# Attention of a hybrid decoder trunk: 20 slots of one head pair become 13 slots of one or two pairs, with the mask buffers at another address

## The chip, the cores and the metric

One core of one Trainium2 chip runs the whole program. The metric is the device time of one execution in microseconds (us).

## What is computed

The reference is a decoder trunk of two layers on 512 tokens of width 1024, in float32. A layer is a SwiGLU feed-forward half step, a mixer of three parallel groups of heads, and a second SwiGLU half step:

```python
x = x + 0.5 * swiglu(rms_norm(x, ffn1_norm[l]), ...)
h = rms_norm(x, mix_norm[l])
(dq, dk, dv, iq, ik, iw, gq, gk, gv, gz, ga, gb, mq) = split_columns(h @ w_in[l])
out_a = dsa_attention(qa, ka, va, q_idx, ik, w_idx, rel_bias)   # 6 heads x 64, top 128 keys, causal, relative bias
out_b = gdn_mixer(gq, gk, gv, gz, ga, gb, ...)                  # 6 heads x 64, gated delta rule
out_c = memory_attention(mq, mem_kv, ...)                       # 4 heads x 64, 256 memory tokens
x = x + concat(out_a, out_b, out_c) @ w_out[l]
x = x + 0.5 * swiglu(rms_norm(x, ffn2_norm[l]), ...)
```

This case is about the stage in which out_a and out_c are computed (logits, softmax, product with the values), and the product with w_out that runs beside it.

## The kernel before

**Float32 products.** Large products are made of three matmuls of rounded operands: weights and activations are split in a high part (wh, XH) and a low part (wl, XL), and the helper `three` issues high*high, high*low and low*high (lines 932 to 934). A unit of weights (1 MB) is loaded into raw[0] or raw[1] by SyncE, rounded into wh (by ScalarE, line 1463, and for two units of this stage by GpSimd, line 899, in halves of 128x1024), and VectorE makes wl from raw and wh (line 1838 for halves).

**The order.** Each engine walks the same list, MIX_ORDER, and issues its own part of each step in that order; semaphores tie the engines together. `_order` writes the list. The attention stage is its last part: steps ("att", slot), between them steps of the output product ("rd", r, c, i: one `three` of 128x512 for output block c), additions of a finished output block to the residual ("ex", line 2152 on VectorE), rounds of the top-k selection of the last token block ("sel", lines 1934 to 1939 on VectorE), and halves of weight splits ("hi" and "lo"). `_early` spreads the first two groups of rounds over the slots, and after the last slot TAIL has the remaining 24 rounds. FIRST_ROUNDS use the results of the delta rule (gzT, split by the "gsplit" steps: XH on ScalarE, line 1696, XL on VectorE, line 2085), SECOND_ROUNDS need those of the memory heads, LAST_ROUNDS those of the masked heads.

**The slots.** A job is one head of one block of 128 queries; a pair is two jobs. There are 8 pairs of memory heads (256 keys each), then 12 pairs of masked heads: three each for blocks 0 to 3, with 128, 256, 384 and 512 keys. Pair p passes through the slots as a pipeline:

- slot p: TensorE makes the logits (line 1384) of both heads in two PSUM banks (0 and 1; 6 and 7 for p = 1); VectorE takes the row maxima (line 2111 for memory heads; line 2107, a fused add of the mask and minimum, for the others).
- slot p+1: ScalarE takes the exponential (line 1712) with the row sum; VectorE inverts the sum (line 2124).
- slot p+2: TensorE transposes the probabilities (line 1359) into banks 2 and 5, ScalarE copies them to pT (line 1729); GpSimd spreads the inverse sums (`spread`, rwide, line 873).
- slot p+3: TensorE transposes rwide (line 1369) and multiplies the values with pT (line 1395), both into bank 3; ScalarE copies both to oA (line 1738).
- slot p+4: GpSimd multiplies them (`normalise`, oN, line 865); where a block is complete, ScalarE (line 1719) and VectorE (line 2118) split it into XH and XL.

The masks of masked heads (`combine`, line 892, comb) are made by GpSimd two slots ahead, in four buffers that share their place with the values and keys of the memory heads, so that the first of them waits for the last memory product (`pool.wait_ge(S["jv_done"], M_JOBS)`).

On TensorE the parts of one slot follow each other as: transposes of pair slot-2, transpose of rwide of pair slot-3, logits of pair slot (these wait until the exponentials or maxima of the pair before are done), values of pair slot-3, then the rounds.

Of the kernel before, what the change touches and what calls it, by code (L numbers as in the profile page):

```python
# [8 lines left out]
F32 = mybir.dt.float32  # L9
# [140 lines left out]
N_SLOTS = N_PAIRS + 4  # L150
IDX_BATCHES = 6

# [8 lines left out]
def _early():  # L161
# [24 lines left out]
def logits_bank(p):  # L186

    return 6 if p == 1 else 0
# [10 lines left out]
def _order():  # L199
# [143 lines left out]
    for p in range(N_SLOTS):  # L343
        order.append(("att", p))
# [5 lines left out]
        if p == 1:  # L350
            pull(9.0)
            put(("hi", 16, 0, KD // 2))
# [8 lines left out]
        if 5 <= p <= 12:  # L361
            sel(1)
        put(*EARLY.get(p, ()))
# [12 lines left out]
                  os_ps=4, os_read=4, or_done=4, op_done=4, jr_done=N_PAIRS, jo_done=N_PAIRS, jx_done=N_PAIRS, jb_done=N_PAIRS, og_done=4, gh_done=3, gl_done=3, cb_done=18, tap_done=9, pr_done=24, ex_done=16, hf_hi=3, hf_lo=3,  # L376
# [28 lines left out]
def job(n):  # L405

    return (n // H_M, H_A + n % H_M) if n < M_JOBS else ((n - M_JOBS) // H_A, (n - M_JOBS) % H_A)


# [9 lines left out]


def masked_count(b, j):

    return H_A * (b - 1) + j + 1
# [113 lines left out]
def hybrid_trunk(nc, xt, memt, cols, strip_table, weights, consts, out):  # L537
    depth = cols.shape[1]

    with ExitStack() as ctx:  # L540
# [37 lines left out]
        with ExitStack() as third:  # L578
            comb = [sb(f"comb{i}", [P, T], F32, third) for i in range(4)]
# [20 lines left out]
        sb("behind_gcol", [P, NB, H_B])  # L600
        beta, gdec, bg, kdec, tmpa, tmpb, tmpc = (gcol[:, i] for i in range(7))
        m8 = sb("m8", [P, 8])
        mxs = sb("mxs", [P, 4])
# [9 lines left out]
        with ExitStack() as third:  # L613
            pT = [sb(f"pT{i}", [P, T], F32, third) for i in range(2)]
# [6 lines left out]
        with ExitStack() as third:  # L621
            at = [sb(f"at{i}", [P, T], F32, third) for i in range(4)]
            pT += [sb(f"pT{i}", [P, T], F32, third) for i in range(2, 4)]
# [16 lines left out]
        with ExitStack() as third:  # L640
            oA = sb("oA", [P, 2, 2, P], F32, third)
            rwide = sb("rwide", [P, 2, 2, DH], F32, third)
            oN = sb("oN", [P, 2, 3, P], F32, third)
# [63 lines left out]
        with nc.Block() as block:  # L707
# [56 lines left out]
            def _(pool):  # L764
                def layer(L):
# [90 lines left out]
                    def normalise(p):  # L856

                        if 0 <= p < N_PAIRS:
                            b, j = job(2 * p)
                            done = phase(2 * p)[2]  # L860
                            c = (j if j < H_A else j - H_A) // 2
                            if c == 0 and done > 1:
                                pool.wait_ge(S["o_lo"], done - 1)
                            pool.wait_ge(S["jo_done"], of("jo_done", p + 1))
                            pool.tensor_tensor(oN[:, done % 2, c, :], oA[:, p % 2, 0, :], oA[:, p % 2, 1, :], ALU.mult
                                               ).then_inc(S["jx_done"], 1)

                    def spread(p):

                        if 0 <= p < N_PAIRS:  # L870
                            b, j = job(2 * p)
                            pool.wait_ge(S["jr_done"], of("jr_done", p + 1))
                            pool.tensor_copy(rwide[:, p % 2], rrec[:, b % 2, j:j + 2].unsqueeze(2).to_broadcast([P, 2, DH])
                                             ).then_inc(S["jb_done"], 1)

                    def combine(p):

                        for n in (2 * p, 2 * p + 1):
                            if n >= N_JOBS:
                                return  # L880
                            b, j = job(n)
                            if b and j < H_A:
                                m = masked_count(b, j)
                                w = P * (b + 1)
                                if m == 1:
# [6 lines left out]
                                pool.tensor_tensor(comb[(m - 1) % 4][:, 0:w], strips[j][:, T - w:], unsel[b][:, :],  # L892
# [27 lines left out]
            def _(pe):  # L920
                def layer(L):
# [170 lines left out]
                    def out_round(r, c, i):  # L1092
# [13 lines left out]
                        if early:  # L1106
                            nth_bank = KD * (rounds is SECOND_ROUNDS) + n
                            dst = bank[early_bank(c, rounds is SECOND_ROUNDS)]
                            if (r, i) in STARTS and nth_bank in (1, 2):
                                pe.wait_ge(S["je_done"], 4)  # L1110
                            if (r, i) in STARTS and nth_bank >= 3:
                                pe.wait_ge(S["ex_done"], of("ex_done", nth_bank - 2))
                        else:
                            dst = bank[n]
                            if (r, i) in STARTS:
                                if n in (0, 1):
                                    pe.wait_ge(S["o_lo"], 2 * NB)
                                    pe.wait_ge(S["je_done" if n == 0 else "jm_done"], N_JOBS)
                                elif n in (2, 5):
                                    pe.wait_ge(S["jp_even" if n == 2 else "jp_odd"], N_PAIRS)  # L1120
# [226 lines left out]
                    def attention(slot):  # L1347
                        p = slot - 2
                        if 0 <= p < N_PAIRS:
                            for e in range(2):  # L1350
                                n = 2 * p + e
                                b, j = job(n)
                                if n == 0:
                                    wait_copied(N_GROUPS - 1)
# [909 lines left out]
```

## Time and profile before

| | |
|---|---|
| median of 3 runs | 2112.43 us (2112.2 to 2112.84) |
| the profiled execution: time | 2112.39 us |
| its span, first to last instruction | 2110.6 us |
| granted TensorE clock over the span | 1.000 |
| attention stage, first logits to the last two rounds before TAIL, layer 1 | 601.76 to 681.11 us |
| the same, layer 2 | 1649.52 to 1728.86 us |

The profile page gives busy times of each engine and the costliest groups; the timeline lists instructions in order, `x4` being four of a kind merged in one row, with the idle time of the engine in front of it and what ended that in brackets. PE is TensorE's matmuls, PEld its weight loads, DVE VectorE, ACT ScalarE, POOL GpSimd. Ends of matmuls are modelled, so distances between starts are what is read for them. A float32 logits, value or transpose product is issued as passes: two rows for one logits or value matmul, one for one transpose.

### The profile page before, as it was taken

The numbers are of one execution on the slowest core, as the hardware profiler recorded it, in microseconds if no ns is written. First come the engines' busy times: TensorE is split into PE (matmuls) and PEld (weight loads), VectorE is DVE, ScalarE is ACT, GpSimd is POOL, SyncE is SP. The second block draws the span as 40 slices with busy tenths as digits, with TensorE's granted clock in tenths as the row PEclk, the third lists the DMA queues.
The fourth block names the chain that finished last, engine by engine and source line by source line (L and its number), as shares of the span: only waits on it lengthen the run. The fifth ranks groups of instructions, "written<-read, shape, count | busy, mean of one in ns | idle before, by whom it ended". The sixth has DMA issues, their size and how long they took to land.

```text
span 2110.6 us, 31901 instructions
## 1 busy us (share of the span) xinstructions
PE 2084.5 (99%) x13097; PEld 1676.8 (79%) x13097; DVE 1034.0 (49%) x1421; ACT 775.9 (37%) x1096; POOL 393.9 (19%) x373
## 2 busy tenths in 40 slices
PE   9999999999999999999999999999999999999999
PEld 7888888877766888888888888887777668888887
DVE  5433333688766533433333433336887665334322
ACT  5222222475546422222232222224755554222211
POOL 1110011105035501101111110121051355111000
PEclk9999999999999999999999999999999999999999
DMA  5222222322111222222222222223212112222222
GB/s 194 87 96 99 95 90 95 127 84 72 47 69 38 100 99 99 99 95 90 95 100 99 99 99 93 93 103 113 80 62 92 41 41 100 99 99 86 94 105 75
DMA packets 30646, 192.41 MB, mean 91 GB/s; under 512 B 3216, under 2 KB 5392, under 8 KB 11984
## 3 DMA queue, kind: packets, MB, share of 16 engines
q1 hardware_dynamic: 30160, 189.80, 25.8%
q8 instruction: 77, 1.26, 0.2%
q10 hardware_dynamic: 384, 1.14, 0.1%
q14 instruction: 25, 0.20, 0.0%
HBM read 188.70 MB, written 2.10 MB: 90 GB/s over the span
## 4 chain that ended last, share of the span: by engine, by line
PE 85%; DVE 8%; ACT 4%; issue 2%; POOL 1%; DMA 0%; SPq 0%; DVEq 0%; ACTq 0%; POOLq 0%
PE psum L932 27%; PE psum L934 26%; PE psum L933 26%; DVE wl L1838 1%; PE psum L1384 1%; PE psum L1395 1%; ACT wh L1463 1%; PE psum L1248 1%; PE psum L1245 1%; PE psum L1359 1%; DVE acc L1921 1%; POOL comb L892 1%; DVE wrk L1936 1%; DVE XL L1853 1%; DVE m L1934 1%
## 5 line engine op out<-in xcount | busy, mean ns | idle before, releaser
L932 PE MATMUL psum<-XH,wh 128*128 128x512 f32 x1904 | 756.3, 397 | 4.9 <-DVE XL L1798 2.2
L933 PE MATMUL psum<-XL,wh 128*128 128x512 f32 x1904 | 741.9, 390 | 0.0
L934 PE MATMUL psum<-XH,wl 128*128 128x512 f32 x1904 | 741.8, 390 | 0.0
L932 PEld LDWEIGHTS psum<-XH,wh 128*128 128x128 f32 x1904 | 357.2, 188 | 103.2 <-issue 24.7
L934 PEld LDWEIGHTS psum<-XH,wl 128*128 128x128 f32 x1904 | 357.4, 188 | 75.6
L933 PEld LDWEIGHTS psum<-XL,wh 128*128 128x128 f32 x1904 | 357.6, 188 | 70.5 <-issue 1.0
L1846 DVE TENSOR_TENSOR wl<-raw,wh 128x2048 fp32r<-128x2048 f32 x88 | 201.7, 2292 | 159.4 <-ACT wh L1468 159.4
L932 PE MATMUL psum<-HH,wh 128*128 128x512 f32 x704 | 273.9, 389 | 0.0
L933 PE MATMUL psum<-HL,wh 128*128 128x512 f32 x704 | 273.9, 389 | 0.0
L934 PE MATMUL psum<-HH,wl 128*128 128x512 f32 x704 | 273.9, 389 | 0.0
L1463 ACT ACTIVATE wh<-raw 128x2048 fp32r<-128x2048 f32 (+1 forms) x84 | 157.3, 1872 | 305.5 <-PE psum L934 305.5
L779 POOL TENSOR_TENSOR sg<-sg,rF 128x512 f32<-128x512 f32 x88 | 113.6, 1293 | 783.5 <-ACT sg L1493 783.5
L1824 DVE TENSOR_TENSOR wl<-raw,wh 128x2048 fp32r<-128x2048 f32 x52 | 122.1, 2347 | 251.3 <-ACT wh L1463 251.2
L1499 ACT ACTIVATE HH<-hf 128x512 f32 (+1 forms) x88 | 55.6, 632 | 328.3 <-DVE hf L1875 328.3
L1468 ACT ACTIVATE wh<-raw 128x2048 fp32r<-128x2048 f32 x88 | 167.4, 1902 | 13.1 <-PE psum L934 13.1
L1493 ACT ACTIVATE sg<-sg 128x512 f32<-128x512 f32 x88 | 55.2, 631 | 292.9 <-DVE sg L1867 292.9
L1867 DVE TENSOR_TENSOR sg<-psum,rF 128x512 f32<-128x512 f32 x88 | 60.1, 687 | 193.5 <-PE psum L934 172.1
L933 PEld LDWEIGHTS psum<-HL,wh 128*128 128x128 f32 x704 | 132.1, 188 | 27.5
L934 PEld LDWEIGHTS psum<-HH,wl 128*128 128x128 f32 x704 | 132.1, 188 | 27.5
L932 PEld LDWEIGHTS psum<-HH,wh 128*128 128x128 f32 x704 | 132.1, 188 | 27.3
L1875 DVE TENSOR_TENSOR hf<-sg,psum 128x512 f32<-128x512 f32 x88 | 60.5, 687 | 134.2 <-PE psum L934 125.8
L701 POOL TENSOR_TENSOR sg<-xT 128x512 f32<-128x512 f32 x40 | 47.8, 1197 | 358.9 <-DVE xT L1890 333.4
(255 smaller groups left out, 1980.1 us busy)
## 6 DMA issues: line engine op xcount, KB each, us to landing
raw<-weights SPq DMA_DIRECT2D x143, 1024.0 KB, 4.8
raw<-weights SPq DMA_DIRECT2D x32, 896.0 KB, 4.4
xT<-xt SPq DMA_DIRECT2D x4, 512.0 KB, 6.3
memT<-memt SPq DMA_DIRECT2D x2, 1024.0 KB, 4.9
out<-xT SPq DMA_DIRECT2D x8, 256.0 KB, 6.0
stripsA<-strip_table SPq DMA_DIRECT2D x2, 768.0 KB, 6.6
raw<-weights SPq DMA_DIRECT2D x2, 512.0 KB, 6.6
stripsB<-strip_table SPq DMA_DIRECT2D x2, 512.0 KB, 7.0
```

The costliest lines, as they stand in the source:

```text
L779: pool.tensor_tensor(sg[fs][:, :], sg[fs][:, :], rF[:, :], ALU.mult).then_inc(S["gr_done"], 1)
L932: pe.matmul(out_ap, a_hi, b_hi, start=first, stop=False)
L933: pe.matmul(out_ap, a_hi, b_lo, start=False, stop=False)
L934: return pe.matmul(out_ap, a_lo, b_hi, start=False, stop=last)
L1463: ins = act.activation(wh[u % 2][:, k0:k1, :], raw[u % 2][:, k0:k1, :], ACT.Copy)
L1468: act.activation(wh[j][:, :, :], raw[j][:, :, :], ACT.Copy).then_inc(S["w_hi"], 1)
L1493: act.activation(sg[fs][:, :], sg[fs][:, :], ACT.Silu).then_inc(S["gs_done"], 1)
L1499: act.activation(HH[:, 2 * i + fs, :], hf[fs][:, :], ACT.Copy).then_inc(S["hh_done"], 1)
L1824: dve.tensor_tensor(wl[u % 2][:, :, :], raw[u % 2][:, :, :], wh[u % 2][:, :, :].bitcast(F32), ALU.subtract).then_inc(S["w_lo"], 1)
L1846: dve.tensor_tensor(wl[j][:, :, :], raw[j][:, :, :], wh[j][:, :, :].bitcast(F32), ALU.subtract).then_inc(S["w_lo"], 1)
L1867: dve.tensor_tensor(sg[fs][:, :], bank[fs][:, :], rF[:, :], ALU.mult).then_inc(S["g_free"], 1)
L1875: dve.tensor_tensor(hf[fs][:, :], sg[fs][:, :], bank[2 + fs][:, :], ALU.mult).then_inc(S["u_free"], 1)
```

## The change

Pairs are gathered in batches. Two neighbouring pairs share a batch, and with it the banks, if both are of the same group of heads and their widths together are at most 512 columns: the 8 memory pairs become 4 batches, the 6 masked pairs of blocks 0 and 1 become 3, and the 6 pairs of blocks 2 and 3 stay alone. What was indexed by pair (slots, semaphores, buffers at, pT, oA, rwide, mxs) is indexed by batch. There are 13 batches and 17 slots where there were 20 and 24.

In a shared batch TensorE issues the same matmuls, both pairs' after each other. VectorE takes the maxima of a memory batch with one instruction for each bank (512 columns, two results) in place of two of 256; the copies to pT and oA and the operations of GpSimd are likewise one instruction of twice the width. The exponentials stay one for each head.

The order changes as well. All gsplit steps and the splits of units 16 and 17's halves up to `hi.17.0.4` and `lo.16.4.8` now come in slot 1, ahead of slot 2's attention; the first rounds come in slots 2 to 6 (they were in 3 to 11), the second from 7 on (were 12), and the 8 remaining selection rounds come in slots 2 to 6 (were 5 to 12). The resulting steps of the first slots, before and after (`mm` and `ev` are the last group of the projection; `rd.r.c.i`):

```
before
att.0 mm sum out | att.1 mm ev hi.16.0.4 | att.2 gsplit.0 hi.16.4.8 lo.16.0.4 gsplit.1
att.3 hi.17.0.4 lo.16.4.8 gsplit.2 rd.0.3.0 rd.0.4.0 rd.0.5.0
att.4 lo.17.0.4 hi.17.4.8 rd.0.3.1 rd.1.3.0 ex.3.0 rd.0.4.1
att.5 sel rd.1.4.0 ex.4.0 rd.0.5.1 | ... one sel, one ex and two or three rd in a slot, to att.11
after
att.0 mm sum out
att.1 mm ev hi.16.0.4 gsplit.0 hi.16.4.8 lo.16.0.4 gsplit.1 hi.17.0.4 lo.16.4.8 gsplit.2
att.2 lo.17.0.4 hi.17.4.8 sel rd.0.3.0 rd.0.4.0 rd.0.5.0 rd.0.3.1 rd.1.3.0
att.3 sel lo.17.4.8 sel ex.3.0 rd.0.4.1 rd.1.4.0 ex.4.0 rd.0.5.1 rd.1.5.0 ex.5.0 rd.0.6.0
att.4 sel sel rd.0.6.1 rd.1.6.0 ex.6.0 rd.0.7.0 rd.0.7.1 rd.1.7.0
att.5 sel sel ex.7.0 rd.0.0.0 rd.0.0.1 rd.1.0.0 ex.0.0 rd.0.1.0 rd.0.1.1
att.6 sel rd.1.1.0 ex.1.0 rd.0.2.0 rd.0.2.1 rd.1.2.0 ex.2.0
att.7 hi.18.0.4 rd.1.3.1 rd.1.4.1 | ... one or two rd in a slot, to att.15
```

The masks go to another place: comb becomes two buffers of 2x512 columns in the space of LT and WT, which the delta rule no longer needs, and the wait for the last memory product is gone.

```diff
+BATCHES = []
+for _p in range(N_PAIRS):
+    if (BATCHES and len(BATCHES[-1]) == 1 and (2 * _p < M_JOBS) == is_mem(-1)
+            and job_width(2 * BATCHES[-1][0]) + job_width(2 * _p) <= T):
+        BATCHES[-1].append(_p)
+    else:
+        BATCHES.append([_p])
...
-    spread(FIRST_ROUNDS, 1, range(3, 12), 0)
-    spread(SECOND_ROUNDS, 1, [*range(12, N_SLOTS - 1), N_SLOTS - 1, N_SLOTS - 1], 1)
-    for slot, part, k0 in ((12, "hi", 0), (13, "lo", 0), (16, "hi", KD // 2), (18, "lo", KD // 2)):
+    late = range(7, N_SLOTS)
+    spread(FIRST_ROUNDS, 1, range(2, 7), 0)
+    spread(SECOND_ROUNDS, 1, [*late, late[-1]], 1)
+    for slot, part, k0 in ((7, "hi", 0), (8, "lo", 0), (9, "hi", KD // 2), (11, "lo", KD // 2)):
...
-    for p in range(N_SLOTS):
-        order.append(("att", p))
+    for slot, p in ((i, s) for i in range(N_SLOTS) for s in PAIR_SLOTS[i]):
+        if p == PAIR_SLOTS[slot][0]:
+            order.append(("att", slot))
...
-        with ExitStack() as third:
-            comb = [sb(f"comb{i}", [P, T], F32, third) for i in range(4)]
...
+        with ExitStack() as third:
+            comb = sb("comb", [P, 2, 2, T], F32, third)
         with ExitStack() as early:
             LT = sb("LT", [P, NB, H_B, DH], F32, early)
...
-                                    pool.wait_ge(S["jv_done"], M_JOBS)
...
-                                if m > 4:
-                                    pool.wait_ge(S["jm_done"], n - 3)
+                                if MASKED[n] > 2:
+                                    pool.wait_ge(S["jm_done"], MAXES_BEFORE[i - 1])
...
+                            for p in BATCHES[i]:
+                                b, j = job(2 * p)
+                                w = job_width(2 * p)
+                                q, k, c = (dqT, dkT, j // 2) if j < H_A else (mqT, mkT, (j - H_A) // 2)
                                 for e, r in enumerate(rows):
+                                    pe.matmul(bank[logits_bank(i) + e][:, off:off + w], q[r, c, b * P:(b + 1) * P], k[r, c, 0:w],
+                                              start=True, stop=True).then_inc(S["jl_done"], 1)
+                                off += w
...
+                            if is_mem(i):
+                                for e in range(2):
+                                    dve.wait_ge(S["jl_done"], JOBS_BEFORE[i + 1] - 1 + e)
+                                    dve.tensor_reduce(mxs[:, i % 2, 2 * e:2 * e + 2],
+                                                      bank[logits_bank(i) + e].rearrange("p (k w) -> p k w", w=NM),
+                                                      AX.X, ALU.max, negate=True).then_inc(S["jm_done"], 1)
...
+                                act.wait_ge(S["jtr_done"], JOBS_BEFORE[i] + (e + 1) * len(BATCHES[i]))
+                                if i >= 2 and e == 0:
+                                    act.wait_ge(S["jv_done"], JOBS_BEFORE[i - 1])
+                                act.activation(pT[i % 2][:, e, 0:bank_width(i)], bank[5 if e else 2][:, 0:bank_width(i)], ACT.Copy
+                                               ).then_inc(S["jp_odd" if e else "jp_even"], 1)
```

## Rows read from the trace of the kernel before

**Rows 1.** The page: busy us (share of the span) of each engine.

```profile
PE 2084.5 (99%) x13097; PEld 1676.8 (79%) x13097; DVE 1034.0 (49%) x1421; ACT 775.9 (37%) x1096; POOL 393.9 (19%) x373
```

**Rows 2.** Windows over the stage in both layers: length, then each engine's busy us.

```profile
601.76:681.11 79.35, 75.44 (x513) 52.84 (x514) 53.25 (x140) 48.94 (x155) 42.85 (x63) 1.00 0.12 41
1649.52:1728.86 79.34, 75.44 (x514) 52.85 (x515) 53.35 (x140) 48.94 (x155) 42.86 (x63) 1.00 0.12 41
```

**Rows 3.** Waits of PE from 600 to 700: total us, times, longest.

```profile
PE psum L1384 <- ACT at L1712: 1.3, 1, 1.3
PE psum L1359 <- ACT pT L1729: 1.2, 1, 1.2
```

**Rows 4.** Timeline of PE over one slot of a memory pair: start, us, instruction.

```profile
623.55 0.60 PE L1359 MATMUL psum<-cst,at 128*128 128x128 f32 x4
623.99 0.27 PE L1369 MATMUL psum<-cst,rwide 128*128 128x128 f32 x1
624.19 0.70 PE L1384 MATMUL psum<-mkT,mqT 64*128 64x256 f32 x4
624.82 0.66 PE L1395 MATMUL psum<-pT,mvN 128*64 128x128 f32 x8
625.41 0.50 PE L932 MATMUL psum<-XH,wh 128*128 128x512 f32 x1
625.74 0.40 PE L933 MATMUL psum<-XL,wh 128*128 128x512 f32 x1
...
627.58 0.60 PE L1359 MATMUL psum<-cst,at 128*128 128x128 f32 x4
```

**Rows 5.** Timeline of PE in slots of 512 keys.

```profile
669.91 1.13 PE L1384 MATMUL psum<-dkT,dqT 64*128 64x512 f32 x4
...
670.97 0.88 PE L1395 MATMUL psum<-pT,dvN 128*64 128x128 f32 x12
...
677.25 1.09 PE L1395 MATMUL psum<-pT,dvN 128*64 128x128 f32 x16
678.28 0.50 PE L932 MATMUL psum<-XH,wh 128*128 128x512 f32 x1
```

**Rows 6.** Timeline of DVE: a split, a selection round, additions from PSUM.

```profile
630.03 1.20 DVE L1838 TENSOR_TENSOR wl<-raw,wh 128x1024 fp32r<-128x1024 f32 x1
631.16 0.69 DVE L1934 MAX8 m<-wrk 128x8 f32<-128x512 f32 x1
...
632.55 0.68 DVE L2152 TENSOR_TENSOR xT<-psum,xT 128x512 f32<-128x512 f32 x1
...
660.84 1.27 DVE L2152 TENSOR_TENSOR xT<-psum,xT 128x512 f32<-128x512 f32 x2
```

**Rows 7.** Groups by line, 600 to 692: busy us, mean ns, idle before.

```profile
L1712 ACT ACTIVATE at<-psum,mxs 128x256 f32<-128x256 f32 x16 | 7.4, 475 | 0.1
```

**Rows 8.** Timeline at the start of the stage, ACT and POOL.

```profile
607.85 0.58 ACT L1528 ACTIVATE dvN<-psum,rcol 128x384 f32<-128x384 f32 x1 [1.94 <-PE psum L934]
607.88 1.04 POOL L899 CAST wh<-raw 128x1024 fp32r<-128x1024 f32 x1 [5.67 <-PE psum L934]
```

**Rows 9.** Timeline of DVE and POOL where their operations overlap.

```profile
610.55 0.67 DVE L2085 TENSOR_TENSOR XL<-gzT,XH 128x512 fp32r<-128x512 f32 x1
611.14 1.31 DVE L1838 TENSOR_TENSOR wl<-raw,wh 128x1024 fp32r<-128x1024 f32 x1
611.32 2.03 POOL L899 CAST wh<-raw 128x1024 fp32r<-128x1024 f32 x1
612.37 1.52 DVE L2085 TENSOR_TENSOR XL<-gzT,XH 128x512 fp32r<-128x512 f32 x1
...
650.65 1.00 POOL L892 TENSOR_TENSOR comb<-stripsA,acc 128x384 f32<-128x384 f32 x1
650.82 1.91 DVE L1838 TENSOR_TENSOR wl<-raw,wh 128x1024 fp32r<-128x1024 f32 x1
651.61 1.99 POOL L892 TENSOR_TENSOR comb<-stripsB,acc 128x384 f32<-128x384 f32 x1
```

More of the change, by code:

```diff
@@ L149, with job, job_width, is_mem @@
 N_PAIRS = N_JOBS // 2
-N_SLOTS = N_PAIRS + 4
 IDX_BATCHES = 6
+def job(n):
+    return (n // H_M, H_A + n % H_M) if n < M_JOBS else ((n - M_JOBS) // H_A, (n - M_JOBS) % H_A)
+def job_width(n):
+    b, j = job(n)
+    return P * (b + 1) if j < H_A else NM
+def is_mem(i):
+    return 2 * BATCHES[i][0] < M_JOBS
+BATCHES = []
[5 more added lines that the diff above has]
+        BATCHES.append([_p])
+N_BATCHES = len(BATCHES)
+N_SLOTS = N_BATCHES + 4
+JOBS_BEFORE = [2 * b[0] for b in BATCHES] + [N_JOBS]
+MAXES_BEFORE = [0]
+for _i in range(N_BATCHES):
+    MAXES_BEFORE.append(MAXES_BEFORE[-1] + (2 if is_mem(_i) else 2 * len(BATCHES[_i])))
+def jobs_of(i):
+    jobs = []
+    for e in range(2):
+        off = 0
+        for k, p in enumerate(BATCHES[i]):
+            w = job_width(2 * p + e)
+            jobs.append((e, k, 2 * p + e, slice(off, off + w)))
+            off += w
+    return jobs
+def bank_width(i):
+    return sum(job_width(2 * p) for p in BATCHES[i])
+MASKED = {}
+for _i in range(N_BATCHES):
+    for _, _, _n, _ in jobs_of(_i):
+        if job(_n)[1] < H_A and job(_n)[0]:
+            MASKED[_n] = len(MASKED) + 1
+PAIR_SLOTS = {}
+for _s in range(N_PAIRS + 4):
+    PAIR_SLOTS.setdefault(next((i for i, b in enumerate(BATCHES) if _s in b), _s - N_PAIRS + N_BATCHES), []).append(_s)
+SLOT_OF_PAIR = {s: i for i, ss in PAIR_SLOTS.items() for s in ss}
 EARLY_BANKS = (4, 6, 7)
@@ L362, in _order @@
             sel(1)
-        put(*EARLY.get(p, ()))
+        if p == PAIR_SLOTS[slot][-1]:
+            put(*EARLY.get(slot, ()))
     put(*TAIL)
@@ L1362, in attention @@
-                        p = slot - 3
-                        if 0 <= p < N_PAIRS:
-                            pe.wait_ge(S["jb_done"], of("jb_done", p + 1))
-                            if p:
-                                pe.wait_ge(S["jo_done"], of("jo_done", p))
+                        i = slot - 2
+                        if 0 <= i < N_BATCHES:
+                            if i == 0:
+                                wait_copied(N_GROUPS - 1)
+                            for q, (e, k, n, cols) in enumerate(jobs_of(i)):
+                                pe.wait_ge(S["je_done"], JOBS_BEFORE[i] + q + 1)
+                                if i and k == 0:
+                                    pe.wait_ge(S["jp_odd" if e else "jp_even"], i)
+                                for c0 in range(cols.start, cols.stop, P):
+                                    mm = pe.transpose(bank[5 if e else 2][:, c0:c0 + P], at[i % 2][:, e, c0:c0 + P],
+                                                      const("ident"))
+                                mm.then_inc(S["jtr_done"], 1)
@@ L1371, in attention @@
-                        p = slot
-                        if p < N_PAIRS:
-                            b, j = job(2 * p)
-                            if p == 1:
+                            for k in range(len(BATCHES[i])):
+                                pe.transpose(bank[3][:, (2 + k) * P:(3 + k) * P],
+                                             rwide[:, i % 2, 2 * k:2 * k + 2].rearrange("p e d -> p (e d)"), const("ident"))
+                        i = slot
+                        if i < N_BATCHES:
+                            if i == 1:
@@ L2088, in attention @@
                     def attention(slot):
[L2090 to L2100 removed]
+                        i = slot
```

284 lines of the change are left out of this document (134 added, 150 removed).

## The prediction, made blind

> **What bounds the kernel now.** I read the page first: TensorE is busy for 99% of the span, no other engine for half of it [rows 1]. So only TensorE's time counts: its stream of passes, what a switch between kinds of passes costs, and its idle time. The windows over the stage show 79.35 and 79.34 us in the two layers with the same busy times [rows 2]; I work out one layer and double it. TensorE idles 79.35 - 75.44 = 3.9 us in a layer's stage. The waits name it: the largest are 1.3 us in front of logits until exponentials are done and 1.2 us in front of transposes until a copy to pT is done [rows 3]. The rest, some 75 us, is passes whose number the change leaves alone.
>
> **Prices on TensorE.** One slot of a memory pair with three rounds takes 623.55 to 627.58, 4.03 us [rows 4]. Its parts, by distances of starts: 4 transposes 0.44 (0.11 each); rwide 0.20; logits of 256 columns 0.63; 8 value passes 0.59; nine passes of 512 columns at 0.23 (625.74 to 627.58 is eight), the first 0.33. Logits of 512 columns take 1.06 and 16 value passes 1.03 [rows 5]. So 256 columns more in a bank cost 0.43 and 8 passes more 0.44; what does not grow is 0.20 for logits, 0.15 for values, 0.09 for rwide (0.20 less a transpose of 0.11) and 0.10 for the first round: 0.54 us of switching in a slot. Seven pairs join another: if the fixed part goes with the group of instructions, 7 x 0.54 = 3.8 us a layer is saved. No row shows two pairs in one group; the bounds are 0.54 and, if logits and values pay theirs for each pair, 0.19 (1.3 us). I take 0.54: value passes already alternate between the two heads at 0.055 each without paying anything.
>
> **The masks' new place** lets GpSimd start its 18 masks in slot 3; before, the first waits for the last memory product. They then stay two slots ahead, and the 1.2 us wait for pT late in the stage [rows 3], whose ScalarE queue stood behind GpSimd's backlog, goes: -1.2 us, bounds 0 and -1.2.
>
> **The joined instructions** on VectorE (a reduction of 512 at about 0.60, as an addition of 512 from PSUM: two take 1.27 with the last one's 0.67 [rows 6]), ScalarE and GpSimd save tenths on engines that are not the bound: nothing on the path. The exponentials of a batch, four at 0.475 [rows 7], take at most 1.9 us; five rounds of 0.70 behind each batch's logits hide them from slot 2 on. Without that cover each batch would cost TensorE a microsecond or so.
>
> **The start of the stage** is where the reordering costs. I follow the queues.
> - Two 4-head logits in place of 2-head ones put 2 x 0.43 us in front of the end of the last projection group. ScalarE's copy of it moves from 607.85 to 608.71, GpSimd's first cast from 607.88 to 608.74 [rows 8]. TensorE transposes batch 0 from 609.35 and has the logits of batch 2 out at 611.4.
> - Then everything waits for VectorE. Ahead of slot 2 it now has gsplit, lo.16, gsplit, lo.16, gsplit: 3 x 0.57 (610.55 to 611.14 with its gap [rows 9]) + 2 x 1.13 (630.03 to 631.16 [rows 6]) = 4.0 us undisturbed, from 609.9. In the same time GpSimd has three more casts of 1.04 (the second begins at 609.7) and rwide of twice the width (0.45, my estimate, between nothing and a cast).
> - These two do not run side by side. A cast issued at 611.32 behind a VectorE subtraction took 2.03 us where 1.04 is usual, so it ran after 612.3; the subtraction issued at 612.37, behind it, took 1.52 and not 0.67; at 650.82 a split took 1.91 behind a mask that had begun, and the next mask 1.99 behind the split [rows 9]. Each waits for the whole of the other, in order of issue. So: cast to 610.76, gsplit to 611.33, cast to 612.37, lo.16 to 613.5, rwide to 613.95, gsplit to 614.5, cast to 615.56, lo.16 to 616.7, gsplit to 617.25. GpSimd adds 3.4 us to VectorE's 4.0.
> - VectorE then has the maxima of batch 2 (1.2), a reciprocal and lo.17.0.4 (1.2), done at 619.7. Behind it stand the selection round and TensorE.
> - TensorE: rd.0.3.0 waits for the first lo.16 until 613.6 (2.2 us from 611.4), three rounds to 615.8, a wait for the second lo.16 until 616.8 (1.0), one round to 617.6, a wait for lo.17.0.4 until 619.8 (2.2), one round to 620.6.
>
> The Trainium skill, SBUF — State Buffer, section "Who interferes with whom", says that a VectorE instruction with two SBUF inputs and a GpSimd one that reads SBUF exclude each other for a whole instruction and that issue order decides who blocks; this speaks against the change. By it the chain ends at 619.7 as above; if the two engines were independent, at about 616.4. The trace agrees with the rule: 2.03 against 1.04.
>
> **Slot 3.** TensorE: 8 transposes 0.87, two rwide 0.31, logits 1.06 to 622.8, values 1.02, four rounds 2.9, to 626.7. rd.0.6.0 needs the bank that ex.3.0 empties. VectorE: maxima of batch 3 from 622.9 to 624.1, reciprocal, sel 1.39 (631.16 to 632.55 [rows 6]), behind GpSimd's rwide 0.25, lo.17.4.8 1.13, sel 1.39, ex.3.0 0.66: 629.0. TensorE idles 2.3 us; rd.0.6.0 ends at 629.85.
>
> **Slots 4 to 15** by the prices, the terms being transposes, rwide, logits, values, rounds:
> - 4: 0.87 + 0.31 + 0.64 + 1.02 + 3.58 = 6.42; 5: 0.87 + 0.31 + 0.85 + 1.02 + 3.58 = 6.63; 6: 0.43 + 0.31 + 1.06 + 1.02 + 2.9 = 5.72. The ex steps are done some 3 us before their banks are wanted.
> - 7: 0.65 + 0.31 + 0.85 + 0.59 = 2.40. Then rd.1.3.1 needs the split of the last memory block, which VectorE has only behind the two maxima of slot 7: two of 384 columns at 0.47 and the split at 0.4, estimated by their columns from the 0.60 of 512, begin 0.1 behind the logits, so about 0.95 idle behind the values; rounds 1.5.
> - 8 to 15, all as in the slots of one pair before: 3.64 + 4.33 + 3.51 + 4.21 + 3.73 + 3.59 + 2.89 + 2.72 = 28.62.
>
> 629.85 + 6.42 + 6.63 + 5.72 + 2.40 + 0.95 + 1.5 + 28.62 = 682.1, where the kernel now is at 681.11 [rows 2]. The same as a sum for a layer: -3.8 switching; -1.2 pT; -2.0 for the other idle time (3.9 less 1.2, less some 0.7 that stays behind ScalarE's copy of the last projection group); +2.2 + 1.0 + 2.2 + 2.3 + 0.95 = +8.65 of new waits; -0.8, because the new waits are counted from the end of streaming and the old ones from the modelled end. +0.85, and +0.95 by the walk. TAIL is the same 24 rounds and what follows shifts rigidly. Two layers: +1.9 us on the profiled execution's own 2112.39 (1.8 above its span, 0.04 below the median of the runs): **2114.3 us**, +0.09%.
>
> **Rivals.**
> - *A, less is lost in the start:* VectorE gets ahead of most casts. For: the split at 611.14, issued before the cast, took 1.31, hardly more than alone, so a tenth earlier for VectorE's first subtraction turns the order. Against: GpSimd always has its next cast issued. Without the 3.4 us, of which 2.85 reach TensorE: 0.95 - 2.85 = -1.9 a layer, 2108.6 us.
> - *B, switching is paid for each pair:* logits and values of the second pair pay 0.20 + 0.15 again, in slots 0 to 6. 7 x 0.35 = 2.45 a layer, all on the path, since even slots 0 and 1 push the casts: +3.4 a layer, 2119.2 us. It decides from 0.17 us for each joined pair, where +0.95 becomes 2.1 a layer. For: a pair's heads lie in different rows of the array, and 0.20 could be the price of changing rows. Against: the value passes.
> - *C, the waits go as well:* VectorE is early throughout; -3.8 - 1.2 = -5.0 a layer, 2102.4 us. Against: the rounds stand in a fixed order behind the splits.
> - *D, nothing moves:* what the passes gain, idle time takes; within the forecast.
>
> **Numbers.** The measurement tells 0.2%, 4.2 us, from no change. Forecast with D 0.45 (0.05 of it beyond +4.2), A 0.22 (0.12 of it below -4.2), B 0.25, C 0.08. Faster 0.08 + 0.12 = 0.20, slower 0.25 + 0.05 = 0.30, same 0.50. C and the far end of B stay out of the range, 2106.5 to 2119.8; the forecast's own is 2111 to 2117.
>
> **What would show it.** Right: rows of DVE for gsplit and wl of 1.5 to 2.2 us between 610 and 618, with casts of POOL as long; waits of PE of 1 to 2 us each for DVE wl before rounds and one for DVE xT between 611 and 630, and again in layer 2; no wait for pT near 655; 4-head logits 1.06 from the next group. Wrong: 4-head logits of 1.25 or more (B); lo.17.0.4 done before 618 (A); waits for ex steps in slots 4 to 6 too.

## The result and the profile after

The change makes the kernel slower: 2119.75 us, the median of six runs (2116.29 to 2122.49), against 2112.48 (2112.2 to 2113.24); the ratio is 1.0033, 95% interval [1.0022, 1.0045]. That is inside the range by 0.05 us, 5.4 us above the forecast, and outside the 0.2% that the prediction called "same". Two things stand out before any trace is opened: the six runs now spread over 6 us where the six before spread over 1, and the mean granted clock of TensorE, 1.000 in the profiled execution before, is 0.998 in the fastest run and 0.996 in the slowest.

The profiled execution is the fastest, 2116.29 us with a span of 2114.5. First the page's busy row, then windows over the stage in both layers, between the same steps as in [rows 2] (first logits, last two rounds before TAIL):

```profile
PE 2080.4 (98%) x13097; PEld 1680.6 (79%) x13097; DVE 1033.0 (49%) x1391; ACT 771.4 (36%) x1054; POOL 386.9 (18%) x347
```

```profile
601.50:682.21 80.71, 73.40 (x513) 54.37 (x514) 52.82 (x125) 47.09 (x135) 39.58 (x50) 0.98 0.12 40
1650.60:1733.02 82.42, 73.73 (x514) 54.46 (x514) 52.76 (x125) 47.21 (x135) 39.60 (x50) 0.98 0.11 39
```

The stage is 1.36 us longer in layer 1 and 3.08 in layer 2; with -0.26 us ahead of the first and -0.28 after it outside the stage these are the 3.90 us between the two profiled executions. TensorE is *less* busy than in [rows 2], by 2.0 and 1.7 us, and idle for 7.3 and 8.7 us instead of 3.9. And the clock is no longer 1.00.

**The waits of TensorE**, layer 1 (from 600 to 700) in the first four rows, layer 2 (from 1650 to 1750) in the last:

```profile
PE psum L984 <- DVE wl L1895: 3.0, 2, 1.8
PE psum L984 <- DVE xT L2215: 2.0, 1, 2.0
PE psum L984 <- issue: 1.0, 1, 1.0
PE psum L1409 <- ACT pT L1787: 0.6, 1, 0.6
...
PE psum L984 <- DVE wl L1895: 4.3, 3, 2.0
```

L984 is the first matmul of a round, so these are the waits that the prediction put in front of rd.0.3.0, rd.0.3.1, rd.1.3.0, rd.0.6.0 and rd.1.3.1 (the last shows as "issue": the round starts at 650.97, when VectorE's split of the last memory block, begun at 650.45, is done). The wait for pT of [rows 3] is halved, not gone.

**VectorE and GpSimd in the start.** The timeline of VectorE, then that of GpSimd:

```profile
609.58 1.46 DVE L2142 TENSOR_TENSOR XL<-gzT,XH 128x512 fp32r<-128x512 f32 x1 [2.06 <-ACT XH L1756]
610.97 2.05 DVE L1895 TENSOR_TENSOR wl<-raw,wh 128x1024 fp32r<-128x1024 f32 x1
612.94 0.88 DVE L2142 TENSOR_TENSOR XL<-gzT,XH 128x512 fp32r<-128x512 f32 x1
613.74 2.05 DVE L1895 TENSOR_TENSOR wl<-raw,wh 128x1024 fp32r<-128x1024 f32 x1
...
617.60 1.19 DVE L1895 TENSOR_TENSOR wl<-raw,wh 128x1024 fp32r<-128x1024 f32 x1
```

```profile
608.48 3.46 POOL L951 CAST wh<-raw 128x1024 fp32r<-128x1024 f32 x3 [6.53 <-PE psum L986]
611.89 1.39 POOL L928 COPY rwide<-rrec 128x256 f32<-128x256 f32 x1
613.23 1.49 POOL L951 CAST wh<-raw 128x1024 fp32r<-128x1024 f32 x1
617.74 1.31 POOL L928 COPY rwide<-rrec 128x256 f32<-128x256 f32 x1 [3.02 <-DVE rrec L2187]
```

A split that is issued while a cast of GpSimd is under way takes 2.05, and the copy and the cast issued while a split is under way grow as well (1.39 and 1.49). The split at 617.60 was issued ahead of GpSimd's copy: it keeps its 1.19, and the copy, 0.14 behind it, takes 1.31. So it is the later one that waits, for the whole of the earlier. The chain ends at 618.8, not 619.7, of which 0.26 is the earlier start of the stage.

**TensorE in the same time**, and behind it windows of 2 us in both layers; the third figure from the end is the granted clock:

```profile
613.07 0.73 PE L984 MATMUL psum<-XH,wh 128*128 128x512 f32 x1 [1.83 <-DVE wl L1895]
613.59 0.63 PE L985 MATMUL psum<-XL,wh 128*128 128x512 f32 x1
614.02 0.63 PE L986 MATMUL psum<-XH,wl 128*128 128x512 f32 x1
...
616.83 0.39 PE L984 MATMUL psum<-XH,wh 128*128 128x512 f32 x1
...
620.83 1.13 PE L1440 MATMUL psum<-mkT,mqT 64*128 64x256 f32 x8
621.89 1.09 PE L1455 MATMUL psum<-pT,mvN 128*64 128x128 f32 x16
622.92 0.50 PE L984 MATMUL psum<-XH,wh 128*128 128x512 f32 x1
```

```profile
612.00:614.00 2.00, 0.93 (x2) 0.77 (x3) 2.00 (x3) 1.39 (x4) 2.00 (x2) 0.79 0.00 0
614.00:616.00 2.00, 2.00 (x6) 1.61 (x5) 2.00 (x2) 0.00 (x0) 0.72 (x1) 0.50 0.00 0
616.00:618.00 2.00, 1.69 (x6) 0.97 (x5) 2.00 (x5) 0.97 (x5) 0.26 (x1) 0.85 0.53 127
...
1666.00:1668.00 2.00, 0.06 (x1) 0.06 (x1) 2.00 (x5) 1.87 (x8) 1.16 (x1) 0.97 0.70 283
1668.00:1670.00 2.00, 2.00 (x6) 1.61 (x7) 1.24 (x3) 0.06 (x1) 1.53 (x3) 0.50 0.49 205
1670.00:1672.00 2.00, 2.00 (x13) 1.78 (x13) 0.00 (x0) 1.20 (x2) 0.00 (x0) 0.67 0.00 0
```

Behind the first long wait the granted clock is 0.50, the 1.2 GHz level: passes of 512 columns start 0.43 us apart where they were 0.23 before and are 0.23 again from 616.83. In layer 1 that cost nothing: the three rounds took 1.6 us more, in time in which the next two splits were awaited anyhow. In layer 2 the clock held through the first wait and fell behind the last; there a round, 8 transposes and the rwide pair take 3.57 us (1667.94 to 1671.51) instead of 0.80 + 0.87 + 0.31 = 1.98, with nothing to hide it. That 1.6 is the difference between the layers, 1.71. So two theories have to be told apart: **the waits and nothing else** (the forecast, with its sizes), and **the waits and the lower clock that follows them**, which costs a varying amount and would make the median exceed the forecast. The kept trace is that of the fastest run; for the five slower ones only the mean clock is on record.

The last rows of the timeline decide rival B: logits of four heads take 1.06 us (620.83 to 621.89) and 16 value passes 1.03, exactly the prices of one wide group in [rows 5].

### The profile page after: what moved, and what is told of

Same layout as the page of the kernel before. It is cut to its first block and busy times, and to the rows that moved or that the text cites. A ratio compares the mean times of both kernels' runs of the same rounds, so it can differ in the third digit from the quotient of the medians.

```text
span 2114.5 us, 31663 instructions
## 1 busy us (share of the span) xinstructions
PE 2080.4 (98%) x13097; PEld 1680.6 (79%) x13097; DVE 1033.0 (49%) x1391; ACT 771.4 (36%) x1054; POOL 386.9 (18%) x347
## 5 line engine op out<-in xcount | busy, mean ns | idle before, releaser
L984 PE MATMUL psum<-XH,wh 128*128 128x512 f32 x1904 | 756.0, 397 | 16.7 <-DVE wl L1895 7.3
L984 PEld LDWEIGHTS psum<-XH,wh 128*128 128x128 f32 x1904 | 357.7, 188 | 113.7 <-issue 21.5
L984 PE MATMUL psum<-HH,wh 128*128 128x512 f32 x704 | 273.9, 389 | 0.0
L984 PEld LDWEIGHTS psum<-HH,wh 128*128 128x128 f32 x704 | 132.1, 188 | 27.2
```

Source lines behind the costliest of these rows:

```text
L984: pe.matmul(out_ap, a_hi, b_hi, start=first, stop=False)
```

## The experiments

"Stage" is the length between the steps of [rows 2], at layer 1 / layer 2, in the profiled execution. Times are medians; the kernel before had 2112.4 to 2112.7 beside them, in 86 executions from 2111.5 to 2115.3 us, the longest of them at a mean clock of 0.998.

| | time, us | ratio to before, 95% | clock of its runs | stage, us |
|---|---|---|---|---|
| before | 2112.5 | | 0.998 to 1.000 | 79.35 / 79.34 |
| changed | 2119.75 | 1.0033 [1.0022, 1.0045] | 0.996 to 0.998 | 80.71 / 82.42 |
| filled waits | 2115.45 | 1.0011 [1.0002, 1.0021] | 0.999, 1.000 | 80.75 / 80.75 |
| casts on ScalarE | 2117.32 | 1.0023 [1.0013, 1.0032] | 0.996 to 0.998 | 81.76 / 82.36 |
| selection later | 2118.43 | 1.0028 [1.0018, 1.0038] | 0.996, 0.997 | 83.23 / 83.29 |
| masks alone | 2111.99 | 0.9996 [0.9987, 1.0005] | 0.999, 1.000 | 78.92 / 78.89 |
| filled, ex.3.0 first | 2112.07 | 0.9999 [0.9990, 1.0008] | 0.998 to 1.000 | 82.02 / 79.04 |
| joined from the fifth pair | 2115.62 | 1.0015 [1.0006, 1.0024] | 0.997 to 1.000 | 80.23 / 81.64 |
| joined from the ninth pair | 2118.38 | 1.0028 [1.0017, 1.0038] | 0.998 | 82.62 / 82.79 |
| two casts on ScalarE, ex.3.0 first | 2108.66 | 0.9982 [0.9973, 0.9991] | 0.999, 1.000 | 77.34 / 77.39 |
| and rounds one slot later | 2107.27 | 0.9973 [0.9961, 0.9984] | 0.998 to 1.000 | 77.33 / 77.21 |
| ex.3.0 first, nothing else | 2113.88 | 1.0008 [0.9999, 1.0017] | 0.996 to 0.998 | 80.45 / 79.00 |
| before, one longer wait | 2122.56 | 1.0047 [1.0033, 1.0061] | 0.997, 0.998 | 83.64 / 85.14 |
| the version with all of it | 2101.21 | 0.9946 [0.9932, 0.9960] | 0.999, 1.000 | 73.93 / 73.93 |

### Is it the idle time that lowers the clock?

**Filled waits.** Useless passes into a bank that is free then:

```diff
+fills = {(0, 3, 0): (6, 1), (1, 3, 0): (7, 1), (0, 6, 0): (7, 2)}
...
+pe.wait_ge(S["jp_even"], batch)
+for _ in range(n):
+    pe.matmul(bank[2][:, :], XH[:, 0, 0:P], XH[:, 0, :], start=True, stop=True)
```

> The changed kernel with passes of no use (128x128 by 128x512 into a free bank) put on TensorE in front of three of its new waits in a layer: 6 before rd.0.3.0, 7 before rd.1.3.0, 7 before rd.0.6.0, 0.23 us each, so 1.4 to 1.6 us in waits of 1.84, 1.16 to 2.3 and 2.05 us. If the idle time is what lowers TensorE's granted clock: no stretch of the stage below 1.00, the three waits shrink by what the passes fill, and the time is that of the walk at full clock, 2114 to 2116.5 us, with the runs within 1 us of each other. If the idle time has nothing to do with the clock: the same slow stretches, runs scattered over some 6 us as in the changed kernel, and 2119.7 us or more, since TensorE only has 40 passes more.

```profile
602.02:682.77 80.75, 76.29 (x534) 56.95 (x535) 52.84 (x125) 47.07 (x135) 39.59 (x50) 1.00 0.12 40
1651.13:1731.88 80.75, 76.29 (x534) 56.95 (x534) 52.76 (x125) 47.07 (x135) 39.59 (x50) 1.00 0.12 40
```

TensorE does 20 passes more in each layer, and the kernel is 4.3 us *faster* than the changed one. Both stages are 80.75 us, layer 1's own length without them: the fills filled, or replaced, waits without shortening the stage, and no slow stretch is left. So the change costs 1.4 us a layer at full clock, and 4.3 us of the 7.3 are the clock. (The runs spread over 2.2 us, not 1 as expected, at 0.999 and 1.000.) One wait of 1.71 us is left, in front of the first fill, and behind it the clock held.

**The kernel before with one longer wait**, to see it without anything of the change:

```diff
-if i == 0 and r < 3:
+if i == 0 and 0 < r < 3:
     pe.wait_ge(S["hf_lo"], of("hf_lo", r + 1))
```

> The kernel before with one wait made longer and nothing else: rd.0.3.0 waits for the second half of unit 16's split too, so TensorE idles some 2.5 us more near 613 (the split ends near 615.7, the round starts at 613.12). At full clock that is 2.4 to 2.5 us a layer, 2112.6 + 4.9 = 2117.5 us. If idle time lowers the granted clock: stretches at 0.50 to 0.85 between 615 and 622 and between 1663 and 1670, where the kernel before has 1.00 everywhere, and 1.5 to 4 us more: 2119 to 2122 us. If the low clock is due to something else in the changed kernel: 1.00 everywhere and 2117.5 us.

```profile
614.94 0.50 PE L932 MATMUL psum<-XH,wh 128*128 128x512 f32 x1 [2.61 <-DVE wl L1838]
...
615.78 0.63 PE L932 MATMUL psum<-XH,wh 128*128 128x512 f32 x1
616.21 0.63 PE L933 MATMUL psum<-XL,wh 128*128 128x512 f32 x1
...
1710.44 0.69 PE L1359 MATMUL psum<-cst,at 128*128 128x128 f32 x4 [1.24 <-ACT pT L1729]
```

```profile
614.00:616.00 2.00, 1.06 (x4) 0.89 (x5) 1.58 (x2) 0.42 (x2) 2.00 (x2) 0.92 0.24 29
616.00:618.00 2.00, 2.00 (x6) 1.54 (x6) 0.00 (x0) 0.00 (x0) 0.48 (x1) 0.50 0.74 291
...
1712.00:1714.00 2.00, 2.00 (x13) 0.96 (x10) 1.19 (x6) 0.68 (x4) 1.07 (x3) 0.50 0.00 0
```

A wait of 2.61 us costs 4.3 us in layer 1 and 5.8 in layer 2, 10 us in all; the time is 0.6 us above the 2119 to 2122 expected of a lower clock. What exceeds 2.6 in a layer is the clock. In layer 2 it fell a second time, at 1711, behind the wait for pT of 1.24 us; the kernel before has the same wait (654.99) at a clock of 1.00. By the starts of the passes that second fall cost 1.6 us, which is the difference of the layers. It is the idle time, then, and not something else in the change. The Trainium skill, TensorE: Matmul & The Clock Gate, section "HAM oscillation — how this bites in real kernels", describes it for waits on transfers: behind a wait the next group of matmuls starts at the lower clock. The trace of the changed kernel agrees in layer 2, with a wait on VectorE: the first passes behind it start 0.59 and 0.43 us apart, at 0.50. The page has it for waits longer than any here: in these runs the clock fell behind waits of 1.24 to 2.82 us. With the longer wait above it fell only 0.8 us after the rounds had begun again.

### What are the waits made of?

**All four casts on ScalarE.**

```diff
-elif step[0] == "hi" and step[1] in (16, 17):
-    round_weights(*step[1:])
...
-if v not in (16, 17):
-    split_hi(U0 + U_MIX + v, k0, k1)
+split_hi(U0 + U_MIX + v, k0, k1)
```

> The changed kernel with the four casts of units 16 and 17 on ScalarE (1.05 us each there) in place of GpSimd, in the same places of the order. If VectorE and GpSimd exclude each other: the XL subtractions take 0.67 and the splits 1.2 us again (now 1.46 and 2.05), lo.17.0.4 is done near 616.8 instead of 618.8, TensorE's waits for wl fall from 3.0 to about 2.6 us with an earlier end, some 2 us a layer less, 2114 to 2117 us. If VectorE's own amount of work sets the end: lo.17.0.4 stays near 618.8 and the time within 1 us of 2119.7. If ScalarE becomes late with the exponentials of batch 1 and 2 (3.2 us of casts in front): new waits of PE for ACT of 1 us or more, 2120 us or more.

```profile
610.08 0.69 DVE L2139 TENSOR_TENSOR XL<-gzT,XH 128x512 fp32r<-128x512 f32 x1 [3.00 <-ACT XH L1754]
610.68 1.22 DVE L1892 TENSOR_TENSOR wl<-raw,wh 128x1024 fp32r<-128x1024 f32 x1
...
615.44 1.19 DVE L1892 TENSOR_TENSOR wl<-raw,wh 128x1024 fp32r<-128x1024 f32 x1
```

```profile
614.84 0.79 PE L982 MATMUL psum<-XH,wh 128*128 128x512 f32 x1 [1.92 <-ACT at L1767]
```

The same VectorE instructions, in the same order, are back at 0.69 and 1.22, and the split of unit 17 ends 15.6 us after the stage's start instead of 17.3. So GpSimd's casts were what lengthened them. With the order of the rows above (the later one waits, the earlier does not grow) this shows that the two engines exclude each other here, as the prediction had it. But ScalarE now begins batch 1's exponentials 2.8 us later, and rd.0.4.0, whose bank they empty, waits 1.92 us for them; behind that the clock falls again. What the first and the third outcome of the expectation name came true together, and the median, between their ranges, is only 2.4 us lower.

**VectorE's queue in front of ex.3.0.** Four kernels. First, all selection moved to slots 4 to 7:

```diff
-if p == 7:
+if p == 9:
     put(("lo", 17, KD // 2, KD))
-if 5 <= p <= 12:
+if 8 <= p <= 15:
     sel(1)
```

> The changed kernel with the eight selection rounds in slots 4 to 7 (they were in 2 to 6) and lo.17.4.8 in slot 4 (it was in 3), so that ex.3.0 stands directly behind the maxima of batch 3 on VectorE. If that queue is what rd.0.6.0 waits for: the wait for xT of 2.0 us is gone in both layers, slot 3 is 2.0 us shorter, and nothing is given back in slots 4 to 8; 2119.7 - 4.1 = 2115.6 us. If GpSimd's masks or the later additions become late by it: the same 2 us reappear as waits for xT or for a maximum in slots 4 to 9, and the time stays at 2119 to 2121 us.

```profile
657.47 0.43 DVE L1996 TENSOR_SCALAR acc<-wrk 128x512 f32<-128x512 f32 x1
```

```profile
657.98 3.43 POOL L944 TENSOR_TENSOR comb<-stripsA,acc 128x512 f32<-128x512 f32 x2 [3.96 <-DVE acc L1996]
```

```profile
663.32 1.15 PE L1409 MATMUL psum<-cst,at 128*128 128x128 f32 x6 [2.48 <-ACT pT L1787]
```

The wait for xT is gone, and another has grown from 0.6 to 2.5: GpSimd can make the masks of block 3 only when the last selection round is done, now at 657.9, and oN, which ScalarE's split and its copy to pT wait for, stands behind them on GpSimd. The time, 2118.43, is just below the second outcome's range, and the wait that came back is not one it named. The selection has a due time at both ends. So the next variants put two rounds in slot 2, where VectorE idles, none in slot 3, and two each in 4 to 6 (`if p in (4, 5) or 8 <= p <= 13`). With the fills (the third left out), then alone:

> The kernel with filled waits, but without the fill before rd.0.6.0, and with VectorE's order changed so that ex.3.0 comes directly behind the maxima of batch 3: two selection rounds in slot 2, none in slot 3, two each in slots 4 to 6, lo.17.4.8 in slot 4. The clock stays at 1.00 as with the fills, so this prices the queue in front of ex.3.0 alone. If it is the cause of the 2.05 us: 2.0 us less in each layer's stage than with filled waits (80.7 us there), 2115.45 - 4.1 = 2111.3 us. If the selection, which now ends 1.4 us later, holds up the masks of block 3 as with all of it later: the wait for pT near 663 grows from 0.6 to 2 us and 2114 us or more.

> The changed kernel with VectorE's order alone changed (two selection rounds in slot 2, none in slot 3, two each in 4 to 6, lo.17.4.8 in slot 4): all four casts on GpSimd, no fills. The wait before rd.0.6.0 (2.05 us) goes, 0.6 us comes back before rd.1.3.1: 1.5 to 1.7 us a layer at equal clock. If the low clock comes from all idle time of the start together: it is rarer or shorter too, 2112.5 to 2115 us. If it comes from the waits before the rounds of slot 2 alone, which stay as they are: 2119.7 - 3.3 = 2116.4 us, with a granted clock of 0.50 still in a stretch between 612 and 622.

At full clock (layer 2 of the filled one) the stage is 79.04 instead of 80.75: 1.7 us for the order of one engine. Of that, 2.05 are gained and 0.65 lost before rd.1.3.1, whose wait has grown from 1.0 to 1.65; the remaining 0.3 us is not traced. In layer 1 of the same execution the clock fell to 0.50 twice, at 613 and 651, behind waits of 1.71 and 1.65 us that layer 2 has as well without a fall, and that stage has 82.02: one gap of a given length does not decide whether it falls. Alone, the order takes 5.9 us off the changed kernel's time, where its waits account for 3.4. The other 2.5 stay unexplained: the clock still falls, in windows from 618 to 622 and from 1662 to 1666, the mean clock of the eleven runs is the changed kernel's 0.997, and they spread from 2111.66 to 2118.0 us. What a fall costs depends on what comes next: that of layer 1 stands ahead of the attention, and the stage has 80.45; that of layer 2 runs into a wait for the next split, and the stage has the 79.00 of full clock.

**Two casts on ScalarE and ex.3.0 first**, no fills; unit 17's casts there, unit 16's on GpSimd:

> All seven pairs joined, no fills, ex.3.0 early as in the variant with filled waits, and the casts of unit 17 (two of four) on ScalarE, so that GpSimd blocks VectorE for two casts and not for four. From the stage of 80.7 us at full clock: less 2.05 for ex.3.0, less 0.7 to 1.5 for the earlier split of unit 17: 77.2 to 78.0 us, 2109 to 2110.5 us if the clock stays at 1.00 for lack of long waits; 2111 to 2115 us if the idle time left in the start (some 2.5 us in three pieces) still lowers the clock for a few us a layer. If ScalarE's queue is too late for the exponentials of batch 1: a wait of PE for ACT before rd.0.4.0 of over 1 us and no gain over 2115 us.

```profile
602.21:679.55 77.34, 71.78 (x513) 53.22 (x514) 51.60 (x125) 48.94 (x137) 36.92 (x48) 1.00 0.12 42
```

The stage is as expected, the time 0.3 us below what was expected at a clock of 1.00, and it is the first version with the batches that beats the kernel before. It is also the cleanest reading of what batching saves.

### What do switching and the masks save?

**Masks alone**, the kernel before with only the masks' place changed and the wait for `jv_done` gone:

> The kernel before with only the masks' place changed: its four mask buffers in the space of LT, and no wait for the last memory product. By the prediction the wait of 1.2 us for pT near 655 goes in each layer: 2112.4 - 2.4 = 2110.0 us. If that wait has another cause than GpSimd's late start, or the time is taken again by masks that collide with splits and additions of VectorE: 2112 to 2113 us, with the wait of 0.6 to 1.2 us still in the waits of PE.

```profile
601.77:680.69 78.92, 75.36 (x513) 52.78 (x514) 53.29 (x140) 49.04 (x155) 42.97 (x63) 1.00 0.12 41
```

0.43 us a layer, not 1.2; the wait for pT stays at 1.0. The chain in front of it is the one that the prediction names. ScalarE before, then ScalarE and GpSimd with the masks alone:

```profile
654.05 0.52 ACT L1719 ACTIVATE XH<-oN 128x384 fp32r<-128x384 f32 x1 [2.44 <-POOL oN L865]
...
653.63 0.52 ACT L1718 ACTIVATE XH<-oN 128x384 fp32r<-128x384 f32 x1 [2.39 <-POOL oN L865]
...
651.19 1.99 POOL L891 TENSOR_TENSOR comb<-stripsB,acc 128x384 f32<-128x384 f32 x1
```

The copy to pT stands behind this split on ScalarE, the split waits for oN, and oN stands behind a mask of 1.99 us on GpSimd (651.61 in [rows 9], here 651.19). What was wrong is that an earlier start of the masks clears this queue. GpSimd had caught up by then in both kernels: the two masks before wait 1.30 and 1.29 us for VectorE's maxima (647.88 and 647.45). The long mask then meets the same split of 1.91 us, issued at 650.82 before and at 650.40 here, and takes 1.99 as before. What that meeting costs by itself no run shows.

**Joined from the fifth and from the ninth pair**, to keep the old start and only add joined pairs (`_p > 4`, `_p > 8` in the condition that makes the batches; first rounds in slots 3 to 8, and 3 to 10):

> The first four pairs stay alone, as before the change, with the splits, casts and first rounds in their old slots; from the fifth pair on neighbours share banks: five joined pairs, 15 slots plus 4, masks in the new place. If each joined pair saves 0.54 us of switching and the loss was all in the start: the masks' variant has a stage of 78.9 us, less 5 x 0.54 is 76.2 us, twice 2.7 us below its 2112.0: 2106.6 us, clock 1.00. If batches bring their own waits further on (exponentials of four heads, later additions): 2109 to 2113 us, with new waits of PE between 625 and 650.

> As the variant that joins from the fifth pair, but all eight memory pairs stay alone and only the six masked pairs of blocks 0 and 1 are joined: three joined pairs. At 0.54 us each 1.6 us a layer below the masks' variant: 2112.0 - 3.2 = 2108.8 us. If the saving is in the memory pairs alone, or the masked pairs' fused maxima (four instead of two between two slots) make TensorE wait: 2111 to 2113 us.

```profile
601.52:681.75 80.23, 72.92 (x514) 52.99 (x515) 53.83 (x131) 47.75 (x141) 41.49 (x54) 1.00 0.12 40
```

Both are slower, and both expectations missed. The busy time says that the saving is there: 75.36 - 72.92 = 2.44 us for five joined pairs at full clock, 0.49 each; with all seven it is 75.36 - 71.78 = 3.58, 0.51 each. But each variant needed an order of its own, and mine put rounds where their splits were not ready: 3.6 us of waits for wl in the fifth-pair variant (rd.0.3.1 had moved from slot 4 to slot 3), and a wait of 2.8 us before rd.1.3.1 in the ninth-pair one. They show the saving in busy time, and that it is worth nothing without the order; of the start they show little.

### The version with all of it

The last two variants follow the waits left in the one with two casts. The first rounds go to slots 2 to 7 and the second from 8, so that attention stands in front of rd.1.3.0 and first rounds cover the last memory split:

> The kernel with two casts on ScalarE and ex.3.0 early, with the first rounds spread over slots 2 to 7 (they were in 2 to 6), the second from slot 8 (7) and the parts of unit 18 one slot later. rd.1.3.0 then stands in slot 3, behind the attention that covers the split of unit 17 (its wait was 1.42 us), and slot 7 has first rounds while VectorE splits the last memory block (the wait before rd.1.3.1 was 1.65 us). If both waits go: a stage of 77.35 - 3.07 = 74.3 us plus what is late next; I expect 75 us, 2108.7 - 4.7 = 2104 us. If slot 3's logits then wait for the exponentials of batch 2, as the logits of slot 3 do in the kernel before: 1 to 1.5 us of that comes back, 2105 to 2107 us. If nothing is gained: 2108.7 us.

Both waits went, and rd.2.3.0 waited 2.06 us instead, for a split of unit 18 that took 2.22 beside GpSimd's masks; the clock fell behind it, and the time is 3.3 us above the 2104 expected for both waits gone. The last one moves that split into VectorE's idle time at the end of slot 8:

```diff
-for slot, part, k0 in ((8, "hi", 0), (9, "lo", 0), (10, "hi", KD // 2), (12, "lo", KD // 2)):
+for slot, part, k0 in ((8, "hi", 0), (10, "hi", KD // 2), (12, "lo", KD // 2)):
     per_slot[slot].insert(0, (part, 18, k0, k0 + KD // 2))
+per_slot[8].append(("lo", 18, 0, KD // 2))
```

> The kernel with the rounds one slot later, with the first half of unit 18's split at the end of slot 8 (it was in slot 9, behind the maxima of that slot, took 2.22 us beside GpSimd's masks and made rd.2.3.0 wait 2.06 us, and in the profiled run the granted clock fell to 0.50 to 0.60 behind that wait). The cast of it is done near 649.2, VectorE is idle from 648.1 to 651.1, so the split fits there. If so: that wait goes, and what is left of idle time in the stage is some 3.5 us, as in the kernel before; the clock stays at 1.00; stage 77.3 - 2.1 - 0.5 to 1.0 for the clock = 74.4 to 75 us, 2112.5 - 2 x 4.6 = 2103 us, with runs within 1.5 us of each other. If the idle time only moves to the next wait (masks of block 3 behind the split): 2105 to 2107 us.

```profile
649.67 1.23 DVE L1900 TENSOR_TENSOR wl<-raw,wh 128x1024 fp32r<-128x1024 f32 x1 [1.21 <-ACT wh L1524]
```

```profile
601.71:675.64 73.93, 71.53 (x514) 53.32 (x514) 51.36 (x125) 48.60 (x137) 37.09 (x48) 1.00 0.13 44
```

```profile
PE psum L985 <- DVE wl L1900: 1.2, 1, 1.2
PE psum L1410 <- ACT dvN L1589: 0.7, 1, 0.7
PE psum L1441 <- ACT at L1770: 0.5, 1, 0.5
```

5.4 us a layer less than before, 11.2 us in all, with five runs within 0.9 us, and 1.8 us below the 2103 expected. The wait for pT, 0.6 in the changed kernel, is gone too. The chain is still there, in the changed kernel and here:

```profile
660.12 0.53 ACT L1779 ACTIVATE XH<-oN 128x384 fp32r<-128x384 f32 x1 [2.92 <-POOL oN L919]
...
652.90 0.53 ACT L1780 ACTIVATE XH<-oN 128x384 fp32r<-128x384 f32 x1 [2.08 <-POOL oN L920]
```

But the slot in which GpSimd begins the two masks in front of oN (655.85 in the changed kernel, 648.52 here) has two rounds where the changed kernel has one, so TensorE comes to the transposes later, when the copy is done. This is read from the rows; no run tests it alone.

## Why the prediction was nearly right in the mechanism and too low

- **Switching, -3.8 us.** Right: 3.6 at full clock (0.51 for each joined pair, 0.54 forecast). Rival B is out. Rival D, that idle time takes what the passes gain, holds and more: 3.6 us gained in a layer, 5.05 lost.
- **The new waits, +8.65.** Right in place and nearly in size. With the -0.8 for the way of counting, which belongs to them, 7.85 were forecast. Forecast 2.2, 1.0, 2.2, 2.3, 0.95; measured in layer 2: 1.83, 0.47, 2.02, 2.05, 1.02, together 7.4. The chain ended at 618.8 instead of 619.7, since rwide and the fourth cast held VectorE up for 0.2 and 0.85 us and not for their whole 0.45 and 1.04.
- **The lock between VectorE and GpSimd.** Right, shown by the casts on ScalarE. The rule of the Trainium skill that was weighed, SBUF — State Buffer, "Who interferes with whom", is what the trace does: 2.05 us against 1.22. Rival A, that VectorE gets ahead, is out.
- **The masks, -1.2.** Wrong, though the wait was read rightly: pT does wait behind GpSimd's backlog. The new place does not clear it, since the masks in question are paced by VectorE's maxima and one of them meets a long split; 0.43 was gained.
- **The sum at full clock** is therefore +1.4 us a layer (80.75 against 79.35) where the walk gave +0.95 to +1.0: 2115.2 us would have been right, and filled waits gave 2115.45. In its terms: 0.2 us less from switching, and an idle time of 80.75 - 71.8 = 8.95 us where 3.9 + 4.65 = 8.55 were forecast. The new waits are 0.45 us smaller than forecast; the 0.7 behind ScalarE's copy of the last projection group stayed, as forecast; 0.6 for pT and some 0.25 in pieces came on top.
- **The step that failed** is the one that is not in the prediction: that passes keep their price. "By the prices", slots 4 to 15 and all rounds were costed at one clock, because [rows 2] has 1.00 over the stage. The change nearly doubled the stage's idle time and put most of it in a few pieces at the start, the granted clock fell behind them, and this cost 4.3 of the 7.3 us. A rival "the waits lower the clock" was missing.
- **That the time is inside the range is luck.** It is inside by 0.05 us, and the upper end was drawn for rival B. The median, 2119.75, even lies 0.5 us from B's 2119.2, whose price did not come true: the time alone would have spoken for B, and only the rows (1.06 us for four heads' logits) and the filled waits tell the two apart.

What stays open: what exactly decides whether the clock falls behind a given wait. The same 1.7 us of idle time did it in one layer and not in the other, and the 2.0 us before rd.0.6.0 never did it in the changed kernel's trace, though behind them it fell in layer 2 with the casts on ScalarE (windows from 1678 to 1682).

## What to carry to other kernels

Work that is joined leaves less of it between two steps of the same chain: after halving the number of slots, walk through each queue again for what stood in front of each step, because the saving in passes (here 3.6 us a layer) is smaller than two such waits. When an engine at 99% begins to wait for two microseconds at a time, cost the passes behind the wait at the lower clock as well; a mean clock of 0.997 is the sign of it. The spread of the runs is a weaker one: 6 us in the changed kernel, but 1.3 in the kernel before with one longer wait, at the same clock. Filling the wait with useless passes is a quick test of it. And give every step of a filler queue (here the selection) its due time at both ends before moving it.

## What the runs showed of the hardware that was not expected

- TensorE's granted clock fell to 0.50 behind waits from 1.24 us (the kernel before with one longer wait, layer 2) to 2.82 us (joined from the ninth pair, layer 1), and stayed there for some 3 us in the changed kernel (613.5 to 616.8, 1667.9 to 1671.5). Twenty useless passes in a layer made the kernel 4.3 us faster.
- The state is not settled by one wait: with identical code it fell in one layer and not in the other, in the same execution. A fall cost 1.6 us where nothing followed to hide it, and nothing where the next split was awaited anyhow.
- GpSimd's copy for rwide (128x256) takes 0.39 us alone and 1.39 beside a VectorE split: short instructions pay for the other's length.
